# A hybrid decoder trunk on one core: a new written-out order for the delta-rule stage, and two row loads moved behind a spill on the SyncE queue

## The reference, cut to what matters

```python
h = rmsnorm(x, norm_mix);  proj = h @ w_in
qkv = silu(causal_dwconv(qkv_in, w_conv_qkv))          # width 4
a_mat = eye(c) + where(strict, beta * kk * decay, 0)    # per chunk and head
sol = triangular_solve(a_mat, rhs)                      # WY form
v_new = u_c - w_c @ s
o_c = (q_c * exp(g_c)) @ s + qk_c @ v_new
s = s * exp(g_last) + (k_c * exp(g_last - g_c)).T @ v_new
o = rmsnorm(o, w_gdn_norm) * silu(z)
y_sc = proj_B * causal_dwconv(proj_C * proj_h, w_conv_sc)
x = x + concat(o, y_sc) @ w_out
x = x + relu(rmsnorm(x) @ w_up) ** 2 @ w_down
x = x + sigmoid(rmsnorm(x) @ w_ple_gate) * (p @ w_ple_proj)
```

## Time and profile before

| what | value |
|---|---|
| median of three runs | 1505.61 us (1501.57, 1505.61, 1510.59) |
| profiled execution, its own time | 1501.57 us |
| span of the profiled execution | 1499.8 us |
| PE busy | 1460.5 us, 97% |
| DVE, ACT, POOL busy | 729.2, 474.6, 247.4 us |
| the mixed stage (fills, L814) | from 128.1 to 510.5 us |
| mean granted clock of TensorE | 0.995 |

### The profile page before, as it was taken

One profiled execution on the slowest core, in us unless ns is written; L12 is line 12 of the kernel. 1 busy time (PEld: TensorE's weight loads), 2 busy tenths in 40 slices (PEclk: granted clock), 3 DMA queues, 4 the chain that ended last, 5 costly groups with the idle time before them and its releaser, 6 DMA issues.

```text
span 1499.8 us, 24673 instructions
## 1 busy us (share of the span) xinstructions
PE 1460.5 (97%) x9324; PEld 1433.6 (96%) x9324; DVE 729.2 (49%) x1313; ACT 474.6 (32%) x854; POOL 247.4 (16%) x306
## 2 busy tenths in 40 slices
PE   7999799999999999999999999999999999998997
PEld 6999798899999899999999999999999999998997
DVE  5676943668674733633333333333433333335525
ACT  6223343333424422632031121312213122135525
POOL 3200312154443733100000000000000000040303
PEclk9999999999999999999999999999999999999999
DMA  7112312312123263111111111111111111112102
GB/s 178 53 34 57 84 46 69 120 32 83 58 57 101 59 128 73 42 47 53 42 43 57 43 43 42 45 54 43 42 53 46 43 43 56 43 42 71 30 29 116
DMA packets 166315, 89.83 MB, mean 60 GB/s; under 512 B 50763, under 2 KB 160267, under 8 KB 166230
## 3 DMA queue, kind: packets, MB, share of 16 engines
q1 hardware_dynamic: 165222, 84.89, 20.6%
q0 software_dynamic: 1008, 3.79, 0.6%
HBM read 77.97 MB, written 10.69 MB: 59 GB/s over the span
## 4 chain that ended last, share of the span: by engine, by line
PE 90%; DVE 4%; issue 2%; POOL 1%; ACT 1%; DVEq 0%; POOLq 0%
PE pg L696 67%; PE pg L814 13%; PE bk L871 1%; DVE act_lo L1974 1%; PE bk L889 1%; PE bk L885 1%; PE bk L1132 1%; POOL act_lo L2297 1%; PE bk L841 1%; PE bk L1022 1%; PE bk L931 0%; PE bk L934 0%; PE bk L902 0%; PE bk L922 0%; PE bk L939 0%
## 5 line engine op out<-in xcount | busy, mean ns | idle before, releaser
L696 PE MATMUL pg<-act_hi,w_hi 128*128 128x352 f32 x1344 | 434.8, 324 | 9.7 <-issue 3.7
L696 PE MATMUL pg<-act_lo,w_hi 128*128 128x352 f32 x1344 | 430.9, 321 | 0.0
L696 PE MATMUL pg<-act_hi,w_lo 128*128 128x352 f32 x1320 | 423.1, 321 | 0.0
L696 PEld LDWEIGHTS pg<-act_hi,w_hi 128*128 128x128 f32 x1344 | 252.1, 188 | 12.9 <-issue 7.4
L696 PEld LDWEIGHTS pg<-act_lo,w_hi 128*128 128x128 f32 x1344 | 252.6, 188 | 0.0
L696 PE MATMUL pg<-u_hi,w_hi 128*128 128x352 f32 x768 | 249.3, 325 | 0.0
L696 PE MATMUL pg<-u_hi,w_lo 128*128 128x352 f32 x768 | 248.9, 324 | 0.0
L696 PE MATMUL pg<-u_lo,w_hi 128*128 128x352 f32 x768 | 247.8, 323 | 0.0
L696 PEld LDWEIGHTS pg<-act_hi,w_lo 128*128 128x128 f32 x1320 | 247.5, 187 | 0.0
L1151 ACT ACTIVATE w_hi<-w_raw 128x1024 fp32r<-128x1024 f32 x111 | 117.0, 1054 | 379.0 <-PE pg L696 320.1
L2338 POOL TENSOR_TENSOR ssq<-ssq,sq 128x352 f32<-128x352 f32 x72 | 76.1, 1066 | 875.2 <-ACT sq L1151 874.5
(11 more groups left out here) (331 smaller groups left out, 1629.8 us busy)
## 6 DMA issues: line engine op xcount, KB each, us to landing
w_raw<-in_w_up SPq DMA_DIRECT2D x32, 512.0 KB, 4.1
w_raw<-in_w_down SPq DMA_DIRECT2D x32, 512.0 KB, 3.4
w_raw<-in_w_in SPq DMA_DIRECT2D x29, 512.0 KB, 4.0
x_tok<-in_x_prompt SPq DMA_DIRECT2D x8, 512.0 KB, 7.5
w_raw<-in_w_out SPq DMA_DIRECT2D x8, 512.0 KB, 4.2
x_col<-in_x_prompt SPq DMA_DIRECT2D x32, 128.0 KB, 2.9
w_raw<-in_w_ple_gate SPq DMA_DIRECT2D x8, 512.0 KB, 4.1
out<-y_tok SPq DMA_DIRECT2D x8, 512.0 KB, 2.8
```

The costliest lines, as they stand in the source:

```text
L696: last = mm(pg[bank][:, 0:TH], w, a, start=i == 0, stop=i == len(terms) - 1)
```

## The change

Two edits. The first replaces `ORDER`: the same 185 steps, the same 1392 fills, other places. The core of it, up to fill 800, before and after, is below. The second is on SP, in the step `vturn 0`: the loads of the decay rows of chunks 2 and 3 (`load_rows`) move from ahead of the fourth store of sample states to behind the wait for the z spills and the load of z.

```diff
-begin 0 0 49; diff 0 0 7; diff 1 0 7; kk 0 0 8; kk 1 0 0; kq 0 0 0; b1 0 0 9; b2 0 0 34; b3 0 0 0; b4 0 0 30;
-kq 1 0 0; turned 0 0 0; turned 1 0 47; y 0 4 0; y 1 4 12; z 0 4 8; z 1 4 13; y 0 5 22; y 1 5 0; z 0 5 40;
-z 1 5 7; y 0 6 0; y 1 6 39; z 0 6 0; z 1 6 3; s_wait 0 0 13; s_begin 0 0 28; s_norm 0 0 0; s_conv 0 0 25;
-s_kk 0 0 14; s_conv 1 0 11; s_xt 0 0 0; s_conv 2 0 5; s_y 0 0 14; s_z 0 0 16; s_state 0 0 10; s_turn 0 0 3;
-s_solve 0 0 19; s_out 0 0 4; s_onorm 0 0 11; s_put 0 0 5; s_put 1 0 6; s_put 2 0 11; s_put 3 0 0; s_put 4 0 4;
-s_put 5 0 16; s_put 6 0 0; s_put 7 0 42; vturn 0 0 3; vturn 1 0 0; diff 2 0 0; diff 3 0 4; kk 2 0 0; kk 3 0 11;
-kturn 0 0 0; kq 2 0 15; b1 2 0 10; b2 2 0 1; b3 2 0 3; b4 2 0 6; into 0 0 37; turned 2 0 7; solve 0 0 6;
-kq 3 0 14; turned 3 0 8; y 2 4 0; update 0 0 12; y 3 4 0; z 2 4 1; z 3 4 6; sum 0 0 3; into 1 0 0; y 2 5 6;
+begin 0 0 51; diff 0 0 3; diff 1 0 6; kk 0 0 27; kk 1 0 0; kq 0 0 6; b1 0 0 2; b2 0 0 15; b3 0 0 0; b4 0 0 0;
+kq 1 0 29; turned 0 0 5; turned 1 0 45; y 0 4 0; y 1 4 21; z 0 4 4; z 1 4 18; y 0 5 0; y 1 5 18; z 0 5 37;
+z 1 5 1; y 0 6 33; y 1 6 0; z 0 6 24; z 1 6 14; s_wait 0 0 0; s_begin 0 0 17; s_norm 0 0 0; s_conv 0 0 28;
+s_kk 0 0 12; s_conv 1 0 15; s_xt 0 0 0; s_conv 2 0 0; s_y 0 0 6; s_z 0 0 0; s_state 0 0 15; s_turn 0 0 6;
+s_solve 0 0 34; s_out 0 0 5; s_onorm 0 0 13; s_put 0 0 1; s_put 1 0 0; s_put 2 0 4; s_put 3 0 0; s_put 4 0 1;
+s_put 5 0 6; s_put 6 0 0; s_put 7 0 42; vturn 0 0 33; diff 2 0 1; diff 3 0 0; vturn 1 0 0; kk 2 0 0; kq 2 0 0;
+kturn 0 0 13; into 0 0 8; kk 3 0 10; solve 0 0 0; b1 2 0 0; b2 2 0 8; b3 2 0 6; b4 2 0 0; kq 3 0 13;
+turned 2 0 1; update 0 0 12; sum 0 0 22; turned 3 0 21; y 2 4 12; y 3 4 0; z 2 4 2; into 1 0 0; norm 0 0 3;
...
                         sp.wait_ge(sm.s_out_made, 2 * (h + 1))
-                        if h == H - 1:
-                            sp.wait_ge(sm.q_o, 1)
-                            load_rows(2)
-                            load_rows(3)
                         sp.dma_start(os_s[0, :, h, :, :].rearrange("b d e -> d b e"), S_in[:, h, :, :]) \
                             .then_inc(sm.sample_states_out, 16)
                     for x in range(2):
                         sp.wait_ge(z_spilled[x], 16 * (NSC // 2))
                     sp.dma_start(qkv[:, H:2 * H, TP:T], z_dram[:, :, TP:T].rearrange("h p t -> p h t")) \
                         .then_inc(sm.zs_loaded, 16)
+                    sp.wait_ge(sm.q_o, 1)
+                    load_rows(2)
+                    load_rows(3)
```

Behind fill 800 the last steps are, before and after:

```diff
-vturn 6 0 5; vturn 7 0 0; into 6 0 1; kturn 6 0 14; solve 6 0 1; update 6 0 0; sum 6 0 1; kturn 7 0 7;
-into 7 0 15; norm 6 0 26; solve 7 0 9; update 7 0 0; sum 7 0 7; scale 6 0 29; norm 7 0 3; scale 7 0 0;
+scale 5 0 4; vturn 6 0 6; vturn 7 0 7; into 6 0 0; kturn 6 0 17; solve 6 0 11; update 6 0 0; sum 6 0 9;
+kturn 7 0 15; into 7 0 5; norm 6 0 20; solve 7 0 11; update 7 0 0; sum 7 0 22; scale 6 0 28; norm 7 0 0;
+scale 7 0 4; tail 0 0 0
```

More of the change, by code:

```diff
@@ L60 @@
-s_put 5 0 16; s_put 6 0 0; s_put 7 0 42; vturn 0 0 3; vturn 1 0 0; diff 2 0 0; diff 3 0 4; kk 2 0 0; kk 3 0 11;
-kturn 0 0 0; kq 2 0 15; b1 2 0 10; b2 2 0 1; b3 2 0 3; b4 2 0 6; into 0 0 37; turned 2 0 7; solve 0 0 6;
-kq 3 0 14; turned 3 0 8; y 2 4 0; update 0 0 12; y 3 4 0; z 2 4 1; z 3 4 6; sum 0 0 3; into 1 0 0; y 2 5 6;
-y 3 5 0; norm 0 0 4; z 2 5 6; kturn 1 0 4; solve 1 0 0; update 1 0 0; z 3 5 12; sum 1 0 6; y 2 6 9; y 3 6 0;
-norm 1 0 0; scale 0 0 0; z 2 6 0; scale 1 0 0; z 3 6 6; vturn 2 0 8; vturn 3 0 3; diff 4 0 0; diff 5 0 6;
@@ L65 @@
[L65 to L69, removed]
@@ L70 @@
-solve 4 0 37; kq 7 0 5; b3 6 0 20; b4 6 0 0; update 4 0 3; turned 6 0 7; sum 4 0 0; turned 7 0 48; y 6 4 9;
-y 7 4 2; z 6 4 0; z 7 4 4; into 5 0 0; norm 4 0 12; y 6 5 3; kturn 5 0 0; y 7 5 0; z 6 5 0; solve 5 0 6;
-update 5 0 0; z 7 5 0; sum 5 0 22; y 6 6 0; y 7 6 1; norm 5 0 0; scale 4 0 0; z 6 6 0; z 7 6 0; scale 5 0 3;
-vturn 6 0 5; vturn 7 0 0; into 6 0 1; kturn 6 0 14; solve 6 0 1; update 6 0 0; sum 6 0 1; kturn 7 0 7;
-into 7 0 15; norm 6 0 26; solve 7 0 9; update 7 0 0; sum 7 0 7; scale 6 0 29; norm 7 0 3; scale 7 0 0;
@@ L75 @@
-tail 0 0 0
+begin 0 0 51; diff 0 0 3; diff 1 0 6; kk 0 0 27; kk 1 0 0; kq 0 0 6; b1 0 0 2; b2 0 0 15; b3 0 0 0; b4 0 0 0;
[3 more added lines that the diff above has]
+s_solve 0 0 34; s_out 0 0 5; s_onorm 0 0 13; s_put 0 0 1; s_put 1 0 0; s_put 2 0 4; s_put 3 0 0; s_put 4 0 1;
@@ new lines @@
+s_put 5 0 6; s_put 6 0 0; s_put 7 0 42; vturn 0 0 33; diff 2 0 1; diff 3 0 0; vturn 1 0 0; kk 2 0 0; kq 2 0 0;
+kturn 0 0 13; into 0 0 8; kk 3 0 10; solve 0 0 0; b1 2 0 0; b2 2 0 8; b3 2 0 6; b4 2 0 0; kq 3 0 13;
+turned 2 0 1; update 0 0 12; sum 0 0 22; turned 3 0 21; y 2 4 12; y 3 4 0; z 2 4 2; into 1 0 0; norm 0 0 3;
+z 3 4 3; kturn 1 0 29; y 2 5 4; y 3 5 0; z 2 5 4; solve 1 0 0; z 3 5 2; update 1 0 5; y 2 6 0; sum 1 0 0;
+y 3 6 9; scale 0 0 0; z 2 6 7; norm 1 0 8; z 3 6 4; scale 1 0 9; vturn 2 0 2; diff 4 0 9; vturn 3 0 5;
@@ new lines @@
+diff 5 0 0; kk 4 0 18; kk 5 0 3; into 2 0 1; b1 4 0 0; b2 4 0 0; kq 4 0 0; b3 4 0 3; b4 4 0 0; kturn 2 0 32;
+solve 2 0 5; turned 4 0 13; kq 5 0 22; turned 5 0 6; update 2 0 0; y 4 4 1; sum 2 0 7; y 5 4 0; z 4 4 0;
+into 3 0 4; norm 2 0 10; kturn 3 0 0; z 5 4 9; y 4 5 4; solve 3 0 0; y 5 5 0; z 4 5 10; update 3 0 0; z 5 5 12;
+sum 3 0 12; y 4 6 0; y 5 6 2; norm 3 0 0; scale 2 0 0; z 4 6 0; z 5 6 0; scale 3 0 11; vturn 4 0 0;
+vturn 5 0 1; diff 6 0 0; diff 7 0 16; kk 6 0 3; kk 7 0 0; into 4 0 5; b1 6 0 6; kturn 4 0 18; b2 6 0 0;
@@ new lines @@
+kq 6 0 23; solve 4 0 27; kq 7 0 0; b3 6 0 4; b4 6 0 0; turned 6 0 13; turned 7 0 0; update 4 0 10; sum 4 0 23;
+y 6 4 0; y 7 4 0; z 6 4 0; into 5 0 0; norm 4 0 0; z 7 4 19; y 6 5 0; kturn 5 0 6; solve 5 0 0; y 7 5 5;
+z 6 5 13; z 7 5 0; update 5 0 0; sum 5 0 11; scale 4 0 0; y 6 6 4; y 7 6 8; z 6 6 4; norm 5 0 0; z 7 6 0;
+scale 5 0 4; vturn 6 0 6; vturn 7 0 7; into 6 0 0; kturn 6 0 17; solve 6 0 11; update 6 0 0; sum 6 0 9;
+kturn 7 0 15; into 7 0 5; norm 6 0 20; solve 7 0 11; update 7 0 0; sum 7 0 22; scale 6 0 28; norm 7 0 0;
```

## The result

The changed kernel takes 1523.8 us (median of 4 runs, 1523.41 to 1524.73), the kernel before 1506.86 in the same comparison (4 runs, 1501.57 to 1510.59). The ratio is 1.0117, with a 95% interval of 1.0103 to 1.0132: slower by 1.2%, 16.9 us, where +7.5 and 1513.1 were forecast. It lies 1.8 us above the upper end of the range. The profiled execution of the changed kernel took 1522.49 us.

A forecast was written before the change was run, and what follows sets the result against it. PE, busy 97% of the span, was taken as the bound, so only its waits and clock count. Terms 1.9 + 0.8 + 0 + 4.1 + 1.7 - 1.0 = +7.5 us on 1505.6 gave 1513.1; range 1503 to 1522.

The forecast's parts named there:

- the clock: Half clock after the 5.6 us stall ahead of kk 3: +1.7 us, between nothing and 3.4.
- the samples: Sample steps s_conv to s_state: +0.8 us for s_y awaiting ACT's copy, 0 for closer packed state groups.
- Rival 3: Clock falls longer, in the samples and after both stalls: +4 to +9 more, 1517 to 1522; chance 0.13.
- The sample products: Groups s_y, s_z, s_state packed closer: same clock fall and cost as before, 0, between -3.4 and +3.4 us.
- The front: Stage start to y 0 4: kq 1 waits 6.4 us for DVE; +1.9 us net, bounds 0 to +4.
- The wait for third 120: In the front at fill 168, PE stands another 4.3 us until DVE empties this third.
- The hand-over: To chunks 2 and 3: late rows make PE stand 5.6 us ahead of kk 3, before 1.5; +4.1 us.
- Rival 1: Rows' delay is hidden, so the hand-over's 5.8 us go: +1.7, 1507.3; chance 0.16 with smaller mixtures.
- The end: End of the stage: earlier comb lets POOL's last h product start sooner; -1.0 us, 0 to -3.0.
- The stretch from 300 us on: Between 300 and 500 us, some steps wider and others packed: 0, with 2 us either way.
- Rival 2: Front's backlog dissolves, thirds emptied in time: -2.3 us, 1503.3; chance 0.09 with beyond.

The follow-up runs named there:

- experiment 2: Changed kernel with the fills between the eight s_put spaced as before: 1516.2 us, ratio 1.0057.
- (4): Kernel before with the eight s_put packed as in the changed kernel, saved fills put behind the last: 1515.4 us, ratio 1.0054.
- experiment 9: Changed kernel with its packed puts made over all 128 rows in place of 32: 1516.83 us, ratio 1.0064.
- experiment 3: Kernel before with only the SP edit (late row loads): 1508.67 us, ratio 1.0022.
- 10: Changed kernel with the SP edit undone and the puts spaced as before: 1509.5 us, ratio 1.0025.
- 12: Kernel before with 6 of the 16 fills behind s_z moved inside s_state: 1505.63 us, ratio 0.9992.
- experiment 7: Changed kernel with front, state-group spacing, put spacing and SP edit all as before, rest of the order new: 1506.24 us, ratio 1.0011.
- 8: Kernel before with 12 fills moved from behind the last put to inside s_state: 1510.37 us, ratio 1.0037.
- experiment 5: Changed kernel with the fills behind s_y, s_z, s_state and s_turn spaced as before: 1521.8 us, ratio 1.0116.
- experiment 11: Changed kernel with only the front (up to turned 1) in its old places: 1523.01 us, ratio 1.0103.
- experiment 1: Changed kernel with the SP edit undone, row loads again ahead of the fourth store: 1515.51 us, ratio 1.0058.
- experiment 6: Changed kernel with vturn 1 ahead of diff 2 and diff 3, rows still late: 1523.34 us, ratio 1.0128.

## Why the prediction was wrong

The waits that it worked out came nearly as it said. What it had wrong was the clock: mainly at the one group of steps that it didn't cost, and by smaller amounts at the state groups and behind the stall of `kk 3`.

**The step that failed: the samples.** The prediction costed `s_conv` to `s_state`, and passed over `s_put`, although its own table had `s_put 7` move from fill 550 to 522. Its words were that matmuls "packed closer give PE no more to do", so the clock counted 0. For the puts this is wrong by 7.7 us in the trace, and by 7.6 (experiment 2), 8.7 (4) and 7.0 us (9) in the runs. What the runs show: these matmuls with 32 of 128 rows, nearly back to back, keep PE busy all the time and come with 17.1 us at 1.2 GHz in all six profiles that have them so; over 128 rows, in the same places, they come with none. Spread between wide fills, as before, they have no low clock over them in five of seven profiles (before and experiments 2, 3, 10 and 12), 3.4 us in experiment 7, and in 8 a fall that had begun ahead of them.

Rival 3, "the clock falls longer", had the kind of loss and nearly its size (1517 to 1522), and it was right in part for the state groups and behind `kk 3`, but it didn't have this place, where most of the loss is. Its price was bounded by 3.4 us for a stall or group; here one stretch alone was 17.1 us long. The earlier trace rows had the hint: a stretch at 0.50 with PE busy for 6.80 of 6.80 us. A fall without idle time means that idle time isn't what to look for, and the next question should have been which other narrow matmuls the change brings together.

The Trainium skill (TensorE: Matmul & The Clock Gate, HAM oscillation) puts re-throttling down to idle gaps of PE, and the penalty to half the throttled time. The penalty agrees: 17.1 us cost 7.7. The cause agrees for the two long stalls, 6.2 and 5.5 us of idle time with a low clock of 6.8 us each; in the puts the trace has no gap, so there the measurement decides, against the rule.

**The sample products (forecast 0, bounds -3.4 to +3.4).** +2.6 in the trace, inside the bounds, with the lower clock twice as long as before. The value 0 rested on "no more to do", the same wrong reason as for the puts. The effect of the spacing is about 3 us, by the profiles named under experiment 5 and not by its times. That their narrowness (8 columns each) is the cause is argued and not shown.

**The front (forecast +1.9).** +1.6 between the two profiles, but the agreement is mostly luck. `kq 1` waited 6.2 us for 6.4. PE's and DVE's timelines of the changed kernel answer to the earlier trace rows; PE first:

```profile
157.07 2.05 PE L862 MATMUL bk<-qkv 128*128 128x128 f32 x8 [6.20 <-DVE PT L1816]
171.21 0.43 PE L813 MATMUL pg<-act_hi,w_hi 128*128 128x352 f32 x1 [0.94 <-DVE pre L1598]
174.65 1.95 PE L870 MATMUL bk<-X,LY 128*128 128x128 f32 x16
```

```profile
150.34 1.23 DVE L1541 TENSOR_TENSOR w_lo<-w_raw,w_hi 128x1024 fp32r<-128x1024 f32 x1 [1.97 <-ACT w_hi L1150]
```

DVE's 2 us of idle time for `w_hi` are there. The wait for third 120 was 0.94 in place of 4.3 us, because the clock fell right behind the first stall (156.6 to 163.4) and PE arrived later: the fall was covered, as the prediction said. Undone, the front gave back only 0.8 us (experiment 11), too little for these runs to tell. The reason is in the old front, whose two waits of 3.1 and 3.2 us the prediction took to leave the clock at 2.4 GHz. That holds in the one execution that it read. Ten us from the end of each wait on, in the profile of before:

```profile
154.20:164.20 10.00, 8.38 (x53) 8.22 (x54) 9.76 (x15) 2.25 (x3) 2.81 (x3) 1.00 0.19 52
168.00:178.00 10.00, 10.00 (x71) 10.00 (x72) 9.89 (x14) 3.69 (x6) 5.69 (x7) 1.00 0.01 2
```

and in that of experiment 3, which has the same front and waits of 3.2 and 3.1 us as well:

```profile
155.60:165.60 10.00, 10.00 (x54) 9.84 (x55) 9.76 (x15) 2.29 (x3) 2.81 (x3) 0.83 0.20 52
169.40:179.40 10.00, 10.00 (x60) 10.00 (x61) 9.05 (x12) 3.28 (x4) 4.64 (x6) 0.83 0.01 2
```

All six experiments with the old front have 6.8 us of low clock in it. From fill 0 to fill 376 the seven profiles with the new front take 88.6 to 89.0 us; with the old one it is 88.5 to 88.7 in experiments 3, 4, 11 and 12, and 87.0 to 87.1 in 7, 8 and before. So the front costs between nothing and 1.9 us, by where the clock falls in the old one.

**The hand-over (forecast 4.1 + 1.7).** The chain of waits held link by link. SP's queue in the changed kernel answers to the earlier trace rows:

```profile
295.81 0.37 SPq L616 DMA_DIRECT2D qkv<-z_spill  x1
296.21 0.98 SPq L568 DMA_DIRECT2D LY<-g_rows  x2
```

and DVE's and ACT's timelines to the earlier trace rows:

```profile
299.83 2.37 DVE L1791 SCALAR_TENSOR_TENSOR LY<-LY,g_tok,m_inc 128x128 f32<-128x128 f32 x8 [8.50 <-DMA LY<-g_rows]
```

```profile
289.01 1.06 ACT L1150 ACTIVATE w_hi<-w_raw 128x1024 fp32r<-128x1024 f32 x1 [0.76 <-PE pg L813]
...
302.24 0.63 ACT L1150 ACTIVATE LY<-LY 128x512 f32<-128x512 f32 x1 [0.60 <-DVE LY L1791]
302.77 1.13 ACT L1150 ACTIVATE qkv<-bk,sqk 128x128 f32<-128x128 f32 x4
```

With zero at 289.0 the rows go out at +7.2 and `diff 2` starts at +10.8 (forecast 7.2 and about 11), and `kk 3` stood 5.5 us for 5.6. The term mis-sized is the clock: 6.8 us at 1.2 GHz, of which 2.9 us was paid (experiment 1), where 1.7 was chosen from bounds of 0 and 3.4; one of the two rows on which the choice stood was of an execution in which the clock happened to hold. Undone, the late rows are 8.3 us (experiment 1), where the forecast has 5.6 + 1.7 = 7.3; net of the 1.5 us that PE waited there before, it is 7.0 by the table for the forecast 5.8. Rival 1, that the delay is hidden, is half true in the old order (experiment 3, 2.0 to 3.7 us) and false in the new one. The prediction named ACT's order as a link, and it was one; that it wasn't the cause took experiment 6.

**The end (forecast -1.0).** About -0.4: PE's waits behind POOL went from 3.0 to 2.4. `comb` did come earlier, but the product of the h unit still stood behind other work of POOL in its timeline:

```profile
517.94 1.29 POOL L2290 TENSOR_TENSOR comb<-comb,rs 128x512 f32<-128x512 f32 x1 [6.91 <-ACT rs L1150]
519.19 0.81 POOL L2233 TENSOR_TENSOR pre<-pre,cv 128x352 f32<-128x352 f32 x1
519.96 1.30 POOL L2326 TENSOR_TENSOR qkv<-qkv 128x512 f32<-128x512 f32 x1
521.22 1.74 POOL L2233 TENSOR_TENSOR pre<-pre,cv 128x320 f32<-128x320 f32 x1
```

**The stretch from 300 us on (forecast 0).** 0, by the steady 21.2 to 21.3 of the table and by experiment 7. Rival 2, the front's backlog dissolving, is false: PE waited 5.4 to 9.3 us for DVE there under every order tried, and 7.9 before.

**What stays open.** Where exactly the clock falls in the front, over the state groups and over spaced puts differs between executions. How closely narrow matmuls may follow one another was not sought, and whether it is the rows as such or what they hold, mostly zeros, was not separated.

## What to carry to other kernels

When an order is changed, list every group of matmuls that uses a small part of the array, by rows and by columns, and see which groups move together; a plan that counts durations and waits doesn't see the price. Deal wide matmuls between narrow ones, or widen the narrow ones if the data allow it. Ahead of a wait, count not only the stall but the slow clock behind it, and before calling a link the cause, ask which other engine carries the same delay. Read the granted clock from more than one execution before you take from it what a wait costs: here the one at hand was 5 us below the median, and its clock held where the others fell.

## What the runs showed of the hardware

- The granted clock was 1.2 GHz with PE busy for 17.10 of 17.10 us in the changed kernel, and held at 2.4 GHz, through the same steps with 1.1 us of idle time, when the same matmuls had 128 rows in place of 32 (experiment 9).
- PE's waits of 3.1 and 3.2 us in the old front came with no fall of the clock in one profile (before) and with two of 3.4 us in four others (experiments 3, 4, 11 and 12).
- A low stretch cost about half its length where PE was busy throughout (7.7 us for 17.1), and less where PE waited during it (2.9 for the 6.8 at `kk 3`).
- The spread of the kernel before goes largely with the granted clock. Over 52 runs of it beside the experiments (1501.9 to 1510.9 us) the mean is 1504.8 us for the 20 at a mean clock of 0.991, 1507.2 for the 13 at 0.990, 1508.6 for the 4 at 0.986, and 1501.9 for the one at 0.995; the correlation is -0.78. The profile from which the prediction was worked out is of the last kind.
